# Gathering finished pairs of expert rows during the last MoE blocks of a hybrid decoder layer

## The chip, the core and the metric

The kernel runs on one core of one Trainium2 chip. The metric is the device time of one execution in microseconds (us), given as the median of several runs. Five engines work side by side: TensorE (PE in the rows, PEld its weight loads), VectorE (DVE), ScalarE (ACT), GpSimd (POOL) and SyncE (SP, which here only issues transfers). The transfers themselves are carried by 16 DMA engines. A transfer issued by SP goes through one queue, an indexed one (indirect) issued by POOL through another.

## What is computed

The reference is one decoder layer over 1024 prompt tokens and 64 sample tokens (1088 rows of 1024 floats). The part that matters here is the end of it, a mixture of 32 experts in which each token goes to the best two experts of its best group:

```
g_idx = top_k(softmax(xt @ rg_w + rg_b), 1)                     # one of 4 groups
v2, e_idx = top_k(le_sel, 2)                                    # two of its 8 experts
w2 = softmax(v2) * p_top
hg, hu = xt @ w_gate[e], xt @ w_up[e]                           # 1024 -> 128
out = sum over the two experts of (silu(hg) * hu * gate) @ w_down[e]
x = x + out
y = x * rsqrt(mean(x * x) + 1e-6) * g_final
```

## The kernel before

All rows are in 9 tiles: tiles 0 to 7 hold 128 prompt tokens each, tile 8 (`LAST`) the 64 sample tokens. The first two thirds of the time go to projections and mixers: 16 column pieces of `w_in` are loaded by SP into two `raw` buffers, each when the piece two before it has been split (`load_piece`), and TensorE reads the split pieces from a ring of four. Then each tile is projected back and routed. VectorE writes, for every expert, the list of its tokens.

The experts run in `NB` = 29 blocks. Blocks 0 to 7 are experts 0 to 7. The other 24 experts are put in an order by their size (`pos`, a position 0 to 23 for each): ten small ones run in pairs, two to a block, then the large ones, then the rest, one to a block. `place(r)` says which expert position block `r` does. For each block, POOL gathers the tokens' rows from `scratch_h` into `xg`, TensorE multiplies them, ScalarE and VectorE each copy half of the result into `outb`, and POOL scatters `outb` to the DRAM tensor `scratch_out` (`scatter`, L1217). That tensor has 2 x 1088 rows of 4 KB, the two rows of a token next to each other, so a token's pair is 8 KB in one piece. A block with up to 128 rows is scattered in one of four sizes, chosen on POOL by branches (`by_size`). SP loads the weights of an expert (3 x 512 KB) into one of eight slots as soon as the slot's last user is done. VectorE does small pieces of bookkeeping between the blocks (`between`, keyed by the block's number).

After block 28 comes code for experts with more rows than fit, which runs zero times on these inputs: a loop of three rounds on TensorE, ScalarE, VectorE and SP (`Fori`), and on POOL `over_from(0)`, one branch around 19 nested levels of code. When both scatter semaphores are full, POOL does a `memset` whose end is `moe_done` (L1270). That releases SP, which loads the pair rows of all nine tiles, whole, in the order `FINAL` = 8, 0, 1, 2, 3, 4, 7, 5, 6 (L652, 0.5 MB for tile 8, 1 MB for each other one).

A tile's end is the same whoever does it: its own rows plus each of its two expert rows times a gate, then a norm. For tiles 8, 1, 3, 7 VectorE adds (`add_experts`, L1961, two instructions). For tiles 0, 2, 4, 5, 6 TensorE adds (`PE_TILES`: first the own rows by the identity, `own_rows`, L2479, then eight matmuls with diagonal gate matrices `dg`, L2496); the own rows of tile 6 come between tiles 4 and 5, as they need the banks of tile 0. ScalarE squares and takes the root in the order of `FINAL` (L669 or L1096, then L1081), VectorE scales (`final_norm`, L1969 and L1974), and SP stores the tile. VectorE's order is written out by hand: add 8, norm 8, add 1, norm 0, 1, 2, add 3, add 7, norm 3, 4, 7, 5, 6.

Of the kernel before, what the change touches and what calls it, by code (L numbers as in the profile page):

```python
# [27 lines left out]
P = 128  # L28
# [30 lines left out]
DVE_TILES = [8, 1, 3, 7]  # L59
NPAR = 31 + 3 + 4  # L60
# [103 lines left out]
def build_layer(nc, a):  # L164
    with ExitStack() as ctx:
# [128 lines left out]
        order = at("order", [P, 8, REST], o_state + 2304)  # L294
        eid = at("eid", [1, REST], o_state + 3072, I32)
# [26 lines left out]
        eidx = sb("eidx", [P, 2, 2])  # L322
# [41 lines left out]
            "eid_ready", "perm_ready", "ones_ready", "place_ready", "table_added", "cols_ready", "idx_ready", "ov_ready", "xg_zero", "three_gathers",  # L364
# [139 lines left out]
        def _(sp):  # L504
# [58 lines left out]
            for g in range(4):  # L563
                q = g % 2 * 64
                sp.dma_start(pw[q:q + 64, g // 2, q:q + 64], a["pool_w"][0, g])\
                    .then_inc(s["pw_in"], 16)
            for p in range(2, NPIECE):
                load_piece(p)
                if p == 5:

                    sp.wait_ge(s["wsT_masked"], 1)
                    for b in range(SB):
                        sp.dma_start(wsb[b * ST:(b + 1) * ST, :, b * ST:(b + 1) * ST],
                                     wsT[0:ST, :, 0:ST]).then_inc(s["wsb_in"], 16)
                if p == 4:

                    sp.wait_ge(s["h_ready"], TILES)
                    sp.dma_start(gain[:], a["g_ffn"].to_broadcast([P, D]))\
                        .then_inc(s["gain_ffn_in"], 16)
                    sp.dma_start(lng[:], a["ln_d_g"].to_broadcast([P, W])).then_inc(s["ln_d_in"], 16)  # L580
                    sp.dma_start(lnb[:], a["ln_d_b"].to_broadcast([P, W])).then_inc(s["ln_d_in"], 16)
# [10 lines left out]
            def expert_block(i, j, e, first=False):  # L592

                if not first:

                    sp.wait_ge(s["d_done"], i * LAP + max(done_in(NE + j - LAP), NB + j - LAP) + 1)
                load_expert(i, j, e, first)
# [507 lines left out]
        def _(pool):  # L1105
# [106 lines left out]
            def scatter(b, index):  # L1212
# [8 lines left out]
                if is_pair(b):  # L1221
# [12 lines left out]
            pool.wait_ge(s["xg_zero"], XG)  # L1234
            for k in range(2):
                pool.wait_ge(h2_stored[k], 16 * ((TILES + 1 - k) // 2))
            pool.wait_ge(s["idx_ready"], 1)
            def gather_over(o):

                with pool.If(total > o):  # L1240
# [5 lines left out]
                    gather(NB + o, gcol[:, o:o + 1], scol[:, o:o + 1], NB + o - 3)  # L1246

            for b in range(-XG, NB + 1):
# [14 lines left out]
                if b >= 1:  # L1263
                    scatter(b - 1, columns(b - 1)[1])

# [20 lines left out]
            over_from(0)  # L1286


        @block.vector
        def _(dve):  # L1290
# [314 lines left out]
            def route(i):  # L1605
# [25 lines left out]
                do(v.tensor_copy(eidx[q, z, :], j8[q, 0:2]))  # L1631

            def places(i):
# [17 lines left out]
                do(stt(col[q, :], eidx[q, z, :], float(CAPB), rhi[q, :], ALU.mult, ALU.add))  # L1651
# [57 lines left out]
            do(v.memset(flat[:], 0.0))  # L1709
            for i in range(LAST):  # L1710
# [154 lines left out]
            def overflow_counts():  # L1865

                do(ts(ovi[:], carry[0:1, :], float(P - 1), None, ALU.add))
# [5 lines left out]
                do(ts(few[0:1, :], pos[0:1, :], LIGHT - 0.5, None, ALU.is_le))  # L1873
                do(stt(again[:, FIX:NE], rest[0:1, :], 64.0, few[0:1, :], ALU.is_gt, ALU.mult))
                do(ts(few[0:1, :], pos[0:1, :], LIGHT + LARGE - 0.5, -1.0, ALU.is_ge, ALU.add))
                do(stt(run[0:1, :], rest[0:1, :], P + 64.5, few[0:1, :], ALU.is_le, ALU.mult))
                do(stt(few[0:1, :], pos[0:1, :], LIGHT - 0.5, run[0:1, :], ALU.is_ge, ALU.mult))
                do(stt(n_e[:, FIX:NE], few[0:1, :], 1.0, n_e[:, FIX:NE], ALU.add, ALU.mult))
                do(tt(n_e, n_e, again[:, 0:NE], ALU.add))
                do(v.tensor_tensor_scan(incl, ones[0:1, 0:NE], n_e, 0.0, ALU.mult, ALU.add))  # L1880
# [3 lines left out]
            def overflow_sums():  # L1884

                do(tt(otmp[:], incl.unsqueeze(1).broadcast_to(grid), iob[:].unsqueeze(2).broadcast_to(grid),
# [3 lines left out]
            def overflow_lists():  # L1890

                do(tt(otmp[:], otmp[:], ovm[:].unsqueeze(1).broadcast_to(grid), ALU.mult))
# [8 lines left out]
            def overflow_blocks():  # L1901
# [4 lines left out]
                do(v.tensor_copy(ovt[:, 2 * OVER:2 * OVER + 1], incl[:, NE - 1:NE]), s["ov_ready"])  # L1906

            between = {1: expert_order, 2: light_columns, 3: extra_columns, 4: other_columns,
# [47 lines left out]
            def add_experts(i):  # L1956

                n = rows(i)
                dve.wait_ge(pair_in[i], 16)
# [32 lines left out]
        def _(pe):  # L1992
# [494 lines left out]
            for t, i in enumerate(PE_TILES):  # L2487
# [3 lines left out]
                pe.wait_ge(pair_in[i], 16)  # L2491
# [38 lines left out]
```

## Time and profile before

| | |
|---|---|
| median of 3 runs | 609.39 us (609.37 to 610.42) |
| the profiled execution's own time | 608.55 us |
| its span, first to last instruction | 606.5 us |
| TensorE busy | 571.4 us, 94% of the span |
| VectorE busy | 439.9 us, 73% |
| POOL busy | 88.5 us, 15% |
| moved by DMA | 111.27 MB, mean 183 GB/s |

Busy time is an average over stages. In the stage of the experts TensorE is busy nearly all the time; in the last 40 us no engine is, and what counts there is which transfer or result comes last. The span ends with the last store. The execution's own time is 2.05 us more than its span; the median of the runs is 0.84 us above the profiled execution.

### The profile page before, as it was taken

The numbers are of one execution on the slowest core, as the hardware profiler recorded it, in microseconds if no ns is written. First come the engines' busy times: TensorE is split into PE (matmuls) and PEld (weight loads), VectorE is DVE, ScalarE is ACT, GpSimd is POOL, SyncE is SP. The second block draws the span as 40 slices with busy tenths as digits, with TensorE's granted clock in tenths as the row PEclk, the third lists the DMA queues.
The fourth block names the chain that finished last, engine by engine and source line by source line (L and its number), as shares of the span: only waits on it lengthen the run. The fifth ranks groups of instructions, "written<-read, shape, count | busy, mean of one in ns | idle before, by whom it ended". The sixth has DMA issues, their size and how long they took to land.

```text
span 606.5 us, 9765 instructions
## 1 busy us (share of the span) xinstructions
PE 571.4 (94%) x3401; PEld 473.4 (78%) x3401; DVE 439.9 (73%) x749; ACT 242.2 (40%) x389; POOL 88.5 (15%) x136
## 2 busy tenths in 40 slices
PE   8899999999999999899999995899997999999775
PEld 6799999997899889688888874777654768887222
DVE  4937997999999696746666658899731667786285
ACT  6642112222212427322222116576322567775443
POOL 4300000200000000100000000433331334431000
PEclk9999999999999999999999997899998999999889
DMA  8761210131112202455422107699989999962697
GB/s 317 150 123 38 69 36 1 36 93 35 36 36 79 105 36 69 114 203 198 157 80 93 54 36 247 215 332 404 392 329 412 407 352 395 394 241 97 209 421 299
DMA packets 52598, 111.27 MB, mean 183 GB/s; under 512 B 10867, under 2 KB 29176, under 8 KB 51449
## 3 DMA queue, kind: packets, MB, share of 16 engines
q1 hardware_dynamic: 44773, 92.18, 43.2%
q0 software_dynamic: 7168, 17.84, 8.2%
q8 instruction: 30, 0.49, 0.3%
q10 hardware_dynamic: 596, 0.50, 0.3%
q14 instruction: 31, 0.25, 0.1%
HBM read 96.36 MB, written 21.86 MB: 195 GB/s over the span
## 4 chain that ended last, share of the span: by engine, by line
PE 51%; DVE 17%; DMA 7%; issue 3%; ACT 2%; SPq 1%; POOL 0%; POOLq 0%; DVEq 0%; ACTq 0%
PE ps L2259 14%; PE ps L2081 9%; PE ps L2425 6%; PE ps L2364 3%; PE ps L2386 3%; PE ps L2400 3%; PE ps L2401 3%; PE ps L2402 3%; DMA at_opair_p<-scratch_out 3%; DMA at_wlater<-in_expert_w_down 3%; DVE at_mixP L1360 3%; PE ps L2496 2%; PE ps L2323 2%; DVE at_hT L1319 1%; DVE at_lnsq L1546 1%
## 5 line engine op out<-in xcount | busy, mean ns | idle before, releaser
L2081 PE MATMUL ps<-at_hT,at_ring 128*128 128x384 f32 x936 | 165.5, 333 | 0.0
L2081 PEld LDWEIGHTS ps<-at_hT,at_ring 128*128 128x128 f32 x936 | 155.9, 188 | 5.1 <-issue 5.0
L2259 PE MATMUL ps<-at_hT,at_mring 128*128 128x512 f32 (+1 forms) x432 | 102.7, 393 | 2.0 <-DVE at_mring L1514 1.3
L2259 PEld LDWEIGHTS ps<-at_hT,at_mring 128*128 128x128 f32 (+1 forms) x432 | 77.3, 182 | 21.3 <-DVE at_mring L1514 1.7
L1360 DVE SCALAR_TENSOR_TENSOR at_mixP<-at_uc,at_par,at_mixP 128x1024 f32<-128x1024 f32 x60 | 77.1, 1285 | 2.1
L2400 PE MATMUL ps<-at_whi,at_hTm 128*128 128x256 f32 x176 | 51.0, 290 | 0.0
L2402 PE MATMUL ps<-at_whi,at_hTm_lo 128*128 128x256 f32 x176 | 49.1, 279 | 0.0
L2364 PEld LDWEIGHTS ps<-sb_ident,at_xg 128*128 128x128 f32 x232 | 29.3, 192 | 18.2 <-issue 15.2
L1795 DVE TENSOR_TENSOR at_wlater_lo<-at_wlater,at_whi 128x1024 fp32r<-128x1024 f32 x30 | 36.7, 1225 | 6.0 <-ACT at_whi L988 5.1
L2425 PE MATMUL ps<-at_wlater,at_actT 128*128 128x512 f32 (+1 forms) x92 | 38.0, 597 | 0.7 <-ACT at_actT L1003 0.7
L988 ACT ACTIVATE at_whi<-at_wlater 128x1024 fp32r<-128x1024 f32 x30 | 31.6, 1055 | 7.3 <-PE ps L2402 6.5
L669 ACT ACTIVATE at_wk<-at_x 128x1024 f32<-128x1024 f32 (+1 forms) x13 | 13.8, 1059 | 51.4 <-DVE at_x L1586 44.8
L2364 PE MATMUL ps<-sb_ident,at_xg 128*128 128x128 f32 x232 | 31.6, 279 | 2.5 <-DMA at_xg<-scratch_h,at_gidxs 2.3
L1777 DVE TENSOR_TENSOR at_hTm_lo<-ps,at_hTm 128x1024 fp32r<-128x1024 f32 x21 | 25.7, 1223 | 11.2 <-ACT at_hTm L969 11.1
L2401 PE MATMUL ps<-at_wlater_lo,at_hTm 128*128 128x256 f32 x120 | 33.6, 280 | 0.0
L2400 PEld LDWEIGHTS ps<-at_whi,at_hTm 128*128 128x128 f32 x176 | 33.1, 188 | 0.2
L2402 PEld LDWEIGHTS ps<-at_whi,at_hTm_lo 128*128 128x128 f32 x176 | 33.0, 188 | 0.0
L1217 POOL DMA_INDIRECT scratch_out<-at_outb,at_sperm x21 | 20.8, 989 | 69.2 <-DVE at_outb L1765 69.2
L1202 POOL DMA_INDIRECT at_xg<-scratch_h,at_gperm x21 | 26.2, 1246 | 20.5 <-issue 14.4
L1765 DVE COPY at_outb<-ps 128x512 f32<-128x512 f32 x29 | 19.9, 686 | 10.6 <-PE ps L2425 10.5
L1012 ACT ACTIVATE at_outb<-ps 128x512 f32<-128x512 f32 x29 | 17.3, 597 | 25.5 <-PE ps L2425 23.2
L2127 PE MATMUL ps<-at_ring,at_hT 128*128 128x256 f32 (+1 forms) x216 | 25.9, 282 | 0.0
(324 smaller groups left out, 919.2 us busy)
## 6 DMA issues: line engine op xcount, KB each, us to landing
at_wlater<-in_expert_w_gate SPq DMA_DIRECT2D x20, 512.0 KB, 11.1
at_wlater<-in_expert_w_up SPq DMA_DIRECT2D x20, 512.0 KB, 12.8
at_wlater<-in_expert_w_down SPq DMA_DIRECT2D x20, 512.0 KB, 15.4
at_raw<-in_w_in SPq DMA_DIRECT2D x16, 512.0 KB, 4.0
at_opair_p<-scratch_out SPq DMA_DIRECT2D x8, 1024.0 KB, 14.7
at_wfirst<-in_expert_w_gate SPq DMA_DIRECT2D x12, 512.0 KB, 9.0
at_wfirst<-in_expert_w_up SPq DMA_DIRECT2D x12, 512.0 KB, 10.0
at_wfirst<-in_expert_w_down SPq DMA_DIRECT2D x12, 512.0 KB, 12.5
```

The lines of the kernel that those rows point to most:

```text
L988: nc.scalar.activation(whi[h][:], half(wexp(w), h), ACT.Copy).then_inc(s[f"w_hi{h}"], 1)
L1202: g.indirect_dma_start(xg[0:n, b % XG, :], None, hs, bass.IndirectOffsetOnAxis(ap=index[0:n, :], axis=0), bounds_check=last_token, oob_is_ ...
L1360: do(stt(y, x, par[:, c, k:k + 1], y, ALU.mult, ALU.add))
L1795: v.tensor_tensor(half(wexp_lo(w), h), half(wexp(w), h), whi[h][:].bitcast(F32), ALU.subtract).then_inc(s[f"w_lo{h}"], 1)
L2081: mm = pe.matmul(ps[:, bank + r, 0:t1 - t0], w[:, wpart, k * P:(k + 1) * P], hT[:, hpart, k, t0:t1], start=(m, wpart, hpart) == (0, 0, 0), ...
L2127: mm = pe.matmul(b[0:n, 0:W].rearrange("p (s c) -> p s c", s=2), hT[:, hpart, k, i * P:i * P + n], vw[:, :, wpart, k * P:(k + 1) * P], sta ...
L2259: mm = pe.matmul(ps[0:n, b + r, :], mring[:, 1 - i % 2, mpart, k * P:k * P + n], wo[:, wpart, k, r * 512:(r + 1) * 512], start=(c, mpart, ...
L2364: mm = pe.transpose(rows_psum(b)[:, k // 4, k % 4 * P:(k % 4 + 1) * P], xg[:, j % XG, :].rearrange("p (q k) -> p k q", k=KC)[:, k, :], ide ...
L2400: pe.matmul(out, x, high, start=k == 0, stop=False)
L2401: pe.matmul(out, x, low, start=False, stop=False)
L2402: mm = pe.matmul(out, x_low, high, start=False, stop=k == KC - 1)
L2425: mm = pe.matmul(ps[n, bank + r, :], actT[:, j % 2, n], wexp(place(j, t or 0))[:, q:q + 512], start=True, stop=True)
```

## The change

The pair rows of six tiles (8, 0, 1, 2, 3, 7) now come through POOL's queue, each in two indexed gathers: an early one for the tokens whose two experts are both done, and a late one for the others. Three waves of two tiles are issued after the scatters of blocks 24, 25 and 26, and wait for the scatters up to block 23, 24 and 25. A list holds for each token its number, or a number beyond the bound, for which nothing is moved: `soon` for the early gathers, `later` for the late ones. The other three tiles (4, 5, 6, `WHOLE`) are loaded whole by SP, once the late gather of tile 1 has landed.

For this, the chosen experts of all tiles are kept (`eidx`), VectorE works out the lists in three new pieces after blocks 11, 12 and 13, the counts of rows over the limit are worked out on all partitions and not on one, SP copies the inputs over `scratch_out` once during the pieces (`fill_out`, ten copies DRAM to DRAM, 8.5 MB), and blocks 25 to 28 are scattered with 128 rows without the branches. The buffers of the pairs and of `dg` move to slots that are free by then.

```
+EARLY = [[8, 0], [1, 2], [3, 7]]
+WAVES = len(EARLY)
+WHOLE = [4, 5, 6]
+def wave_after(n):
+    return NB - 3 - WAVES + n
...
             for p in range(2, NPIECE):
                 load_piece(p)
+                if 5 <= p < 14:
+                    fill_out(p - 5)
...
-            sp.wait_ge(s["moe_done"], 1)
-            for i in FINAL:
-                n = rows(i)
-                src = orow[2 * i * P:2 * (i * P + n), :].rearrange("(t k) d -> t (k d)", k=2)
-                sp.dma_start(opair(i)[0:n, :], src).then_inc(pair_in[i], 16)
+            sp.wait_ge(pair_in[FINAL[2]], 32)
+            for i in WHOLE:
+                src = orow[2 * i * P:2 * (i + 1) * P, :].rearrange("(t k) d -> t (k d)", k=2)
+                sp.dma_start(opair(i), src).then_inc(pair_in[i], 16)
...
-                if is_pair(b):
+                if is_pair(b) or NB - 4 <= b < NB:
                     move(P)
...
+            def pair_rows(i, index):
+                g.indirect_dma_start(opair(i), None, pairs,
+                                     bass.IndirectOffsetOnAxis(ap=index[:, i:i + 1], axis=0),
+                                     bounds_check=last_token, oob_is_err=False).then_inc(pair_in[i], 16)
+            def early_pairs(n):
+                pool.wait_ge(s["turns_ready"], 1)
+                for k in range(2):
+                    pool.wait_ge(scat[k], 16 * ((wave_after(n) + 2 - k) // 2))
+                for i in EARLY[n]:
+                    pair_rows(i, soon)
...
                     scatter(b - 1, columns(b - 1)[1])
+                if 0 <= b - 2 - wave_after(0) < WAVES:
+                    early_pairs(b - 2 - wave_after(0))
...
             over_from(0)
+            pool.wait_ge(s["moe_done"], 1)
+            for i in FINAL:
+                if i not in WHOLE:
+                    pair_rows(i, later)
...
+            def pair_turns():
+                do(v.memset(turn[:, 0:FIX], 0.0))
+                do(v.tensor_copy(turn[:, FIX:NE], pos))
+                shape = [P, TILES * 2, NE]
+                do(tt(w, io32[:].unsqueeze(1).broadcast_to(shape), chosen, ALU.is_equal))
+                do(tt(w, w, turn[:].unsqueeze(1).broadcast_to(shape), ALU.mult))
+            def pair_latest():
+                do(v.tensor_reduce(latest[:], both[:], AX_X, ALU.add))
+                do(tt(done_by[:], latest[:, :, 0], latest[:, :, 1], ALU.max))
+                do(ts(no_over[:], incl[:, NE - 1:NE], 0.5, None, ALU.is_le))
+                do(ts(token[:], pid[:, :, 0], 0.5, -0.5, ALU.mult, ALU.add))
+            def pair_lists():
+                for n in range(WAVES):
+                    last_turn = place(wave_after(n)) - FIX + 0.5
+                    for i in EARLY[n]:
+                        do(ts(done_by[:, i:i + 1], done_by[:, i:i + 1], last_turn, no_over[:], ALU.is_le,
+                              ALU.mult))
+                do(stt(later[:], done_by[:], float(NONE), token[:], ALU.mult, ALU.add))
+                do(ts(done_by[:], done_by[:], -float(NONE), float(NONE), ALU.mult, ALU.add))
+                do(tt(soon[:], done_by[:], token[:], ALU.add), s["turns_ready"])
...
-                pe.wait_ge(pair_in[i], 16)
+                pe.wait_ge(pair_in[i], 16 if i in WHOLE else 32)
```

On POOL, the program's end reads as follows before the change; the first row stands in the last scatter's choice of a size, and the last rows are the end of `over_from`.

```order
L1217 DMA scratch_out<-at_outb,at_sperm 2176x1024
L1194 UNCONDITIONAL_BRANCH
...
L1192 COMPARE_AND_BRANCH
L1217 DMA scratch_out<-at_outb,at_scol 2176x1024
L1192 UNCONDITIONAL_BRANCH
L1217 DMA scratch_out<-at_outb,at_scol 2176x1024
L1194 UNCONDITIONAL_BRANCH
L1270 MEMSET at_gcol 128x1
L1280 UNCONDITIONAL_BRANCH
```

The same place after the change begins with the last scatter (now without branches) and `all_scattered`. The branch L1322 is row 854 of POOL's program and leads around `over_from` to row 1588, the first late gather.

```order
L1244 DMA scratch_out<-at_outb,at_sperm 2176x1024
L1330 COMPARE_AND_BRANCH
L1316 MEMSET at_gcol 128x1
L1330 UNCONDITIONAL_BRANCH
L1322 COMPARE_AND_BRANCH
...
L1316 MEMSET at_gcol 128x1
L1326 UNCONDITIONAL_BRANCH
L1280 DMA at_opair_a<-scratch_out,at_later 128x2048 x4
L1280 DMA at_opair_b<-scratch_out,at_later 128x2048 x2
L173 UNCONDITIONAL_BRANCH
```

Nothing stood behind `over_from` before; six gathers stand there now.

On SP, the last transfers before the change are nine loads and nine stores.

```order
L640 REGISTER_ALU
L640 COMPARE_AND_BRANCH
L652 DMA at_opair_s<-scratch_out 64x2048
L652 DMA at_opair_p<-scratch_out 128x2048 x8
L498 DMA out_y_sample<-at_x_86 64x1024
L498 DMA out_y_prompt<-at_x_86 128x1024 x8
```

After it, three loads are left (L679), and they wait for tile 1's late gather and no longer for `moe_done`.

```order
L668 REGISTER_ALU
L668 COMPARE_AND_BRANCH
L679 DMA at_opair_b<-scratch_out 128x2048 x3
L515 DMA out_y_sample<-at_x_86 64x1024
L515 DMA out_y_prompt<-at_x_86 128x1024 x8
```

Six of nine loads have left SP's queue for POOL's. Earlier on SP, among the pieces, the copies (L589) stand behind the piece loads (L541):

```order
L541 DMA at_raw<-in_w_in 128x8x128
L589 DMA scratch_out<-in_x_prompt 16x16384
L599 DMA at_wsb<-at_wsT 8x4x8 x8
L541 DMA at_raw<-in_w_in 128x8x128
L589 DMA scratch_out<-in_x_prompt 16x16384
L541 DMA at_raw<-in_w_in 128x8x128
L589 DMA scratch_out<-in_x_prompt 16x16384
```

So a piece's load now follows the copy that was issued with the piece before it.

## Rows read from the trace of the kernel before

**Rows 1.** Chain that ended last, in order of time, last 45 us: start, us, what
```profile
567.31 0.09 POOL at_gcol L1270
...
570.11 16.12 DMA at_opair_p<-scratch_out
...
591.68 1.72 PE ps L2479 x4
593.39 6.88 PE ps L2496 x16
```

**Rows 2.** Timeline of VectorE at the end: start, us, what, [idle before <-releaser]
```profile
567.00 0.19 DVE L1947 TENSOR_REDUCE sb_stage<-sb_stage 128x9 f32<-128x36 f32 x1 [4.45 <-issue]
...
572.59 2.59 DVE L1961 SCALAR_TENSOR_TENSOR at_x<-at_opair_s,sb_gates,at_x 64x1024 f32<-64x1024 f32 x2 [4.51 <-DMA at_opair_s<-scratch_out]
576.86 0.15 DVE L1969 RECIPROCAL sb_rs<-sb_rs 64x1 f32<-64x1 f32 x1 [1.68 <-ACT sb_rs L1081]
...
585.60 0.16 DVE L1969 RECIPROCAL sb_rs<-sb_rs 128x1 f32<-128x1 f32 x1 [1.48 <-ACT sb_rs L1081]
...
598.47 0.16 DVE L1969 RECIPROCAL sb_rs<-sb_rs 128x1 f32<-128x1 f32 x1 [1.54 <-ACT sb_rs L1081]
...
601.90 0.16 DVE L1969 RECIPROCAL sb_rs<-sb_rs 128x1 f32<-128x1 f32 x1 [1.95 <-ACT sb_rs L1081]
602.10 1.28 DVE L1974 SCALAR_TENSOR_TENSOR at_x<-ps,sb_rs,sb_gain 128x1024 f32<-128x1024 f32 x1
```

**Rows 3.** Timeline of TensorE at the end
```profile
565.64 8.99 PE L2479 MATMUL ps<-at_x,sb_ident 128*128 128x512 f32 x16 [3.82 <-issue]
574.92 3.70 PE L2496 MATMUL ps<-at_opair_p,at_dg 128*128 128x512 f32 x8 [0.29 <-DMA at_opair_p<-scratch_out]
580.26 3.70 PE L2496 MATMUL ps<-at_opair_p,at_dg 128*128 128x512 f32 x8 [1.64 <-DMA at_opair_p<-scratch_out]
586.28 5.40 PE L2496 MATMUL ps<-at_opair_p,at_dg 128*128 128x512 f32 x8 [2.32 <-DMA at_opair_p<-scratch_out]
```

**Rows 4.** Stretches: start:end, length, busy us of PE, PEld, DVE, ACT, POOL, clock, DMA, GB/s
```profile
551.00:563.30 12.30, 10.08 (x52) 6.48 (x50) 5.89 (x8) 4.69 (x9) 2.81 (x3) 1.00 0.27 97
...
580.30:586.30 6.00, 3.68 (x9) 1.42 (x9) 4.22 (x7) 2.85 (x6) 0.00 (x0) 1.00 1.03 425
586.30:594.00 7.70, 7.70 (x14) 3.32 (x15) 7.45 (x8) 3.61 (x7) 0.00 (x0) 0.78 1.00 412
```

**Rows 5.** Timeline of POOL: the first gathers of the experts' stage, and the last scatters
```profile
380.12 1.31 POOL L1202 DMA_INDIRECT at_xg<-scratch_h,at_gidxs  x1 [10.35 <-DVE at_gidxs L1746]
381.74 1.31 POOL L1202 DMA_INDIRECT at_xg<-scratch_h,at_gidxs  x1 [0.30 <-issue]
...
560.50 0.92 POOL L1217 DMA_INDIRECT scratch_out<-at_outb,at_sperm  x1 [3.04 <-DVE at_outb L1765]
563.34 0.92 POOL L1217 DMA_INDIRECT scratch_out<-at_outb,at_sperm  x1 [1.92 <-DVE at_outb L1765]
```

**Rows 6.** Issue to landing: first the two gathers of [rows 5], then L652's nine loads
```profile
DMA to landing us min/median/max: 4.4/4.5/4.7
...
DMA to landing us min/median/max: 5.0/13.2/22.0
```

**Rows 7.** Timeline of VectorE in blocks 7 to 14
```profile
432.68 0.77 DVE L1888 TENSOR_REDUCE at_ovb<-at_otmp 1x19 f32<-1x608 f32 x1
...
466.36 0.29 DVE L1757 TENSOR_TENSOR at_actv<-at_sg,ps 128x128 f32<-128x128 f32 x1 [7.45 <-ACT at_sg L995]
...
469.92 1.23 DVE L1777 TENSOR_TENSOR at_hTm_lo<-ps,at_hTm 128x1024 fp32r<-128x1024 f32 x1 [1.46 <-ACT at_hTm L969]
...
477.10 1.22 DVE L1777 TENSOR_TENSOR at_hTm_lo<-ps,at_hTm 128x1024 fp32r<-128x1024 f32 x1 [0.79 <-ACT at_hTm L969]
```

**Rows 8.** The pieces: two loads of L524 (60 to 71 us), and ScalarE's waits for them
```profile
L524 SPq DMA_DIRECT2D at_raw<-in_w_in x2: 590/600/611, 62.4 to 69.0; - x2
...
ACT at_ring L694 <- DMA at_raw<-in_w_in: 8.5, 2, 5.3
```

More of the change, by code:

```diff
@@ L294, in build_layer @@
         order = at("order", [P, 8, REST], o_state + 2304)
+        both = at("both", [P, TILES, 2, NE], o_state)
+        turn = at("turn", [P, NE], o_state + 2304)
+        latest = at("latest", [P, TILES, 2], o_state + 2304 + 192)
+        done_by = at("done_by", [P, TILES], o_state + 2304 + 288)
+        token = at("token", [P, TILES], o_state + 2304 + 384)
+        soon = at("soon", [P, TILES], o_state + 2304 + 480, I32)
+        later = at("later", [P, TILES], o_state + 2304 + 672, I32)
+        no_over = at("no_over", [P, 1], o_state + 2304 + 736)
         eid = at("eid", [1, REST], o_state + 3072, I32)
@@ L566, in _, with fill_out @@
                     .then_inc(s["pw_in"], 16)
+            def fill_out(n):
+                r = n * 256 % NP
+                for src, at_, count in ((a["x_prompt"][0, r:r + 256, :], n * 256, 256),) if n < 8 else tuple(
+                        (a["x_sample"].rearrange("b t d -> (b t) d"), 2 * NP + h * NS, NS) for h in range(2)):
+                    sp.dma_start(orow[at_:at_ + count, :], src).then_inc(s["out_filled"], 16)
             for p in range(2, NPIECE):
                 load_piece(p)
+                if 5 <= p < 14:
+                    fill_out(p - 5)
                 if p == 5:
@@ L1709, in _ @@
             do(v.memset(flat[:], 0.0))
+            do(v.memset(eidx[:], 0.0))
             for i in range(LAST):
@@ L1865, in overflow_counts @@
             def overflow_counts():
-                do(ts(ovi[:], carry[0:1, :], float(P - 1), None, ALU.add))
+                do(ts(ovi[:], carry[:], float(P - 1), None, ALU.add))
                 do(ts(ovi[:], ovi[:], 7, None, ALU.logical_shift_right))
@@ L1872, in overflow_counts @@
                 do(v.memset(again[:], 0.0))
[L1873 to L1878, printed above, removed]
+                do(ts(few, pos, LIGHT - 0.5, None, ALU.is_le))
+                do(stt(again[:, FIX:NE], rest, 64.0, few, ALU.is_gt, ALU.mult))
+                do(ts(few, pos, LIGHT + LARGE - 0.5, -1.0, ALU.is_ge, ALU.add))
+                do(stt(run, rest, P + 64.5, few, ALU.is_le, ALU.mult))
+                do(stt(few, pos, LIGHT - 0.5, run, ALU.is_ge, ALU.mult))
+                do(stt(n_e[:, FIX:NE], few, 1.0, n_e[:, FIX:NE], ALU.add, ALU.mult))
                 do(tt(n_e, n_e, again[:, 0:NE], ALU.add))
-                do(v.tensor_tensor_scan(incl, ones[0:1, 0:NE], n_e, 0.0, ALU.mult, ALU.add))
+                do(v.tensor_tensor_scan(incl, ones[:, 0:NE], n_e, 0.0, ALU.mult, ALU.add))
                 do(tt(ovm[:], n_e, again[:, 1:NE + 1], ALU.add))
```

41 lines of the change are left out of this document (24 added, 17 removed).

## The prediction

> **What bounds the kernel now.** I read the chain of waits first, from its end backwards. The span of 606.5 us ends with the store of tile 6, 3.1 us behind VectorE's last scaling (602.10 + 1.28 = 603.38) [rows 2]. Ahead of that stand TensorE's sums of tiles 5 and 6 and the own rows of tile 6, and ahead of tile 4's sum 16.12 us of the pair loads [rows 1]. The reader is to see that nothing but these loads stands between `moe_done` (the memset, 567.31) and TensorE's start on tile 4. TensorE's timeline says the same: idle for 0.29, 1.64 and 2.32 us before tiles 0, 2 and 4, each time for a pair load [rows 3]. From 580.3 to 586.3 the DMA engines are busy for all of their time at 425 GB/s [rows 4]: the end is bound by 8.5 MB through the DMA engines. Ahead of it, from 551 to 563.3, they are busy 0.27 of the time [rows 4]. So the change takes bytes from a full stretch to a nearly empty one. VectorE comes next: from its first add at 572.59 to 603.38 it has 30.8 us, of which 1.68, 1.48, 1.54 and 1.95 us stand before roots [rows 2]. That leaves about 24.0 us of work.
>
> **How much moves.** I ran the reference's routing on its inputs and the kernel's ordering of experts over it. Of the 704 tokens in the six tiles, 481 have both experts done when their wave is sent (35, 75, 91, 83, 91, 106 in the order 8, 0, 1, 2, 3, 7) and 223 are late (29, 53, 37, 45, 37, 22). At 8 KB a pair the late gathers carry 1.8 MB; with 3 MB for the whole tiles the end moves 4.8 MB in place of 8.5.
>
> **The end, step by step.** `moe_done` stays at 567.4, the end of the memset [rows 1]. Behind it POOL must branch around `over_from`, some 730 rows of its program, before it can issue a gather. The trace has no such branch on POOL. Bounds: nothing, and the 4.45 us that VectorE spent from its last copy to its next instruction, over its empty loop of three rounds [rows 2]; TensorE spent 3.82 us on its own [rows 3]. POOL has one branch where they have three rounds, so I take the middle, 2.2. The Trainium skill ("Runtime: NRT & Kernel Launch", Instruction fetch mechanics) says that a taken branch out of the two pages held must first fetch the page it leads to; by it alone the price can't be nothing, and the trace agrees in that two engines idle there.
>
> The first late gather (tile 8) is issued at 567.4 + 2.2 = 569.6. Two gathers in a row start 1.62 us apart (380.12, 381.74) [rows 5], so tile 0 follows at 571.2 and tile 1 at 572.8. Landing took 4.4 to 4.7 us from the issue for 128 rows of 4 KB [rows 6], and at the last scatter, issued at 563.34 and waited for by the memset, 3.9 [rows 1, 5]. For 29 to 53 rows of 8 KB (0.24 to 0.43 MB) I take 4.0 to 4.2, with 3.5 and 5.5 as bounds. Tile 8 lands at 573.6, against 572.59 before: a late gather saves nothing for the first tile. Tile 1 lands at 577.0.
>
> Then SP issues the three whole loads. Alone, the 0.5 MB of tile 8 landed in 5.0 us [rows 6]; another 0.5 MB at 425 GB/s adds 1.3, and the late gathers of tiles 2, 3 and 7 (0.85 MB, 2 us of DMA time) go on beside it, for which I add half, 1.0. Tile 4 lands at 577.1 + 7.3 = 584.4, against 586.2 before: 1.8 us earlier. The Trainium skill ("DMA: Bandwidth & Descriptors", Anatomy of one DMA) gives 2.0 us plus bytes at 436 GB/s for one DMA. An estimate by that page: a late gather lands in 2.7 us and 1 MB in 4.4, and tile 4 would be some 3.4 us earlier still; the rows are longer for both.
>
> Two chains lead on from there. **TensorE's:** before, from the start of tile 4 to the end of the span it took 606.5 - 586.28 = 20.2 us. In it are 5.40 us for tile 4's eight matmuls where tiles 0 and 2 took 3.70 [rows 3], in a stretch with a granted clock of 0.78 of full [rows 4], a mean of the levels 2.4 and 1.2 GHz. If the clock falls again, the span ends at 584.4 + 20.2 = 604.6; if it doesn't, 1.7 us earlier. TensorE idled 2.3 us before tile 4 then and would again (tile 2's pairs land at 578.5, its sum ends at 582.2), but it was less busy before that; I take the middle, 603.7. **VectorE's:** 573.6 + 24.0 + 1.7 for the root of tile 8 + 0.1 = 599.4, plus 3.1 for the store = 602.5. With the pairs on hand its other three stalls are gone. The later chain counts: 603.7, 2.8 us less than 606.5. TensorE's first own rows end at 574.63 whatever comes (565.64 + 8.99) [rows 3]. Five sums of 3.5, the own rows of tile 6 with 1.7 [rows 1], a root with 1.6, a norm with 1.5 and the store come behind: even instant pairs don't end below some 600.
>
> **What is hidden.** VectorE's lists. A reduce of 608 elements took 0.77 us [rows 7], so the piece after block 11 costs about 2 us (two operations on 576 elements), the next 1.4, the last some 1.9 (nine small ones). The first falls ahead of the 7.45 us in which VectorE idles until 466.36, the second into the 1.46 us ahead of 469.92; the third has only 0.79 us ahead of 477.10 and moves that instruction by about 1.1 [rows 7]. That one makes the left-over half of a block's rows, which TensorE reads a block later, so I count nothing; if the cover is gone it costs 1.1. The wider counts have the same elements per partition, so no more time.
>
> The early gathers are issued behind scatters that stand over 5 us apart. Only the last wave touches something: its two issues, from 557.5 on, end at about 560.7, and the scatter of block 27 was at 560.50 [rows 5]. Its 1.6 MB are 3.8 us of DMA time in the same queue as the last two scatters. I count 0.2, within 0 and 1.5. Taking the branches away saves nothing, as POOL waited 1.92 us for VectorE at the last scatter [rows 5].
>
> The copies. 1 MB at 425 GB/s takes 2.5 us, or 5 if it counts twice, read and written. The shortest gap that I found between a load with a copy behind it and the next load is 62.4 to 69.0, 6.6 us [rows 8]. Cost nothing, while a copy stays under that.
>
> **Sum.** 606.5 - 2.8 + 0.2 = a span of 603.9, and 605.9 with the 2.05 us around it, 2.6 below the profiled 608.55. The median of the runs is 0.84 above that execution, so 609.39 - 2.6 = 606.8. A measurement of this kernel tells 0.2% from no change, 1.2 us.
>
> **Rivals.**
> A, the forecast: TensorE's chain through the whole loads ends last, 1.2 to 4.2 us gained, median 605.2 to 608.2. Chance 0.55.
> B: the branch costs 0 to 1, or the transfers land up to 3 us sooner. Tile 4 is in by 582, and VectorE's chain or TensorE's floor ends last, at 600.9 to 602.2: 4.3 to 5.6 gained, median 603.8 to 605.1. For it: one branch, and DMA engines with little else to do. Against: two engines idle about 4 us at that place. 0.22. The skill's fit of a DMA, above, leads here.
> C: the branch costs as much as VectorE's 4.45. Tile 4 lands at 586.7 and the end is at 606.9, less up to 1.7 by the clock. Within 0.2%: no change, 608.2 to 610.6. 0.14.
> D, slower: the copies hold the pieces. ScalarE waits twice for a load already, 8.5 us in all [rows 8]; there each us beyond 6.6 a copy is passed on. At 10 us a copy that is 2 x 3.4 = 6.8 lost, less the gain of 2.6: median about 613.6. It decides from 8.5 us a copy on. Against: the copies' bytes are few for 6.6 us. 0.07.
> The last 0.02: the lists come out empty, so that nothing is early, and 8.5 MB go at the end again, six tiles by POOL and with the branch ahead: about 2 us slower.
>
> **How the numbers follow.** Faster by over 0.2%: A and B, 0.77. Same: C and a little of D, 0.15. Slower: 0.08. The range takes in A and most of B and C: 604.0 to 609.0.
>
> **What would show it.** On the span after: tile 8's first add near 573.6 and tile 4's sum near 584.4 for the two landings; between POOL's memset and its first late gather, the price of the branch (2.2). DMA well over 0.27 busy from 551 to 563. No idle on TensorE during the pieces and none new in blocks 12 to 15. The prediction is wrong if the first late gather comes before 568.5 or after 571.5, if the first whole load takes under 5 or over 9 us, or if `moe_done` is displaced by more than 1 us.

## The result, and the profile after

| | before | after |
|---|---|---|
| median of 20 runs each | 609.38 us (607.73 to 611.85) | 612.56 us (610.71 to 614.88) |
| ratio | | 1.0055, 95% interval 1.0042 to 1.0068 |
| profiled execution | 608.55 us, span 606.5 us | 613.24 us, span 611.3 us |

The change made the kernel 3.2 us slower, where 2.6 us of gain were forecast; 612.56 lies outside the range of 604.0 to 609.0. The profiled pair differs by 4.7 us, 1.5 more than the medians.

The page of after, its queues (packets, megabytes, share of the 16 DMA engines):

```profile
q1 hardware_dynamic: 44293, 95.33, 43.9%
q0 software_dynamic: 8960, 23.61, 11.1%
```

So the early gathers and the copies' bytes are there. Between 200 and 345 us the two agree (TensorE busy for 143.0 and 143.4 us, DMA share 0.33 in both), and between 30 and 200 us only the copies' bytes show: TensorE was busy for 168.68 us of those 170 before and is for 168.69 now, while the DMA engines' share rose from 0.20 to 0.31. Columns as in [rows 4]:

```profile
30.00:200.00 170.00, 168.69 (x1104) 162.45 (x1104) 148.23 (x177) 44.07 (x88) 4.58 (x4) 1.00 0.31 106
...
550.00:555.00 5.00, 5.00 (x35) 4.04 (x34) 4.32 (x5) 3.66 (x6) 2.83 (x3) 1.00 0.78 265
555.00:560.00 5.00, 5.00 (x34) 3.99 (x34) 3.30 (x5) 2.41 (x5) 2.46 (x4) 1.00 0.85 276
560.00:565.00 5.00, 4.15 (x12) 1.56 (x11) 0.98 (x2) 1.04 (x3) 3.64 (x4) 1.00 0.91 297
565.00:570.00 5.00, 0.00 (x0) 0.00 (x0) 1.62 (x6) 0.60 (x1) 0.99 (x1) 1.00 0.87 313
```

The stretch ahead of `moe_done`, 0.27 busy before [rows 4], is 0.78 to 0.91 busy now, and at 265 to 313 GB/s, not 425. POOL's timeline there, against [rows 5]: L1244 is a scatter, L1280 a gather of pairs, `soon` the early and `later` the late ones.

```profile
559.59 1.02 POOL L1244 DMA_INDIRECT scratch_out<-at_outb,at_sperm  x1 [1.93 <-DVE at_outb L1816]
560.91 1.02 POOL L1280 DMA_INDIRECT at_opair_b<-scratch_out,at_soon  x1 [0.30 <-issue]
562.24 1.00 POOL L1280 DMA_INDIRECT at_opair_b<-scratch_out,at_soon  x1 [0.30 <-issue]
563.58 1.01 POOL L1244 DMA_INDIRECT scratch_out<-at_outb,at_sperm  x1 [0.34 <-issue]
566.90 0.99 POOL L1244 DMA_INDIRECT scratch_out<-at_outb,at_sperm  x1 [2.31 <-DVE at_outb L1816]
573.76 0.10 POOL L1316 MEMSET at_gcol<- 128x1 int32 x1 [5.87 <-DMA scratch_out<-at_outb,at_sperm]
577.13 1.03 POOL L1280 DMA_INDIRECT at_opair_a<-scratch_out,at_later  x1 [3.27 <-issue]
578.47 1.01 POOL L1280 DMA_INDIRECT at_opair_a<-scratch_out,at_later  x1 [0.31 <-issue]
```

Two things are to be seen. The last scatter (566.90) is waited for until 573.76, 6.9 us, where it was 4.0 from issue to memset before [rows 1, 5]. And 3.27 us of "issue", a wait for nothing that the profile shows, stand between the memset and the first late gather: the way around `over_from`.

VectorE and TensorE of after, against [rows 2, 3]:

```profile
565.42 0.69 DVE L1816 COPY at_outb<-ps 128x512 f32<-128x512 f32 x1 [2.63 <-DMA scratch_out<-at_outb,at_sperm]
...
581.87 2.59 DVE L2040 SCALAR_TENSOR_TENSOR at_x<-at_opair_a,sb_gates,at_x 64x1024 f32<-64x1024 f32 x2 [13.05 <-DMA at_opair_a<-scratch_out,at_later]
586.13 0.15 DVE L2048 RECIPROCAL sb_rs<-sb_rs 64x1 f32<-64x1 f32 x1 [1.68 <-ACT sb_rs L1108]
...
593.82 0.16 DVE L2048 RECIPROCAL sb_rs<-sb_rs 128x1 f32<-128x1 f32 x1 [0.42 <-ACT sb_rs L1108]
...
606.89 1.28 DVE L2053 SCALAR_TENSOR_TENSOR at_x<-ps,sb_rs,sb_gain 128x1024 f32<-128x1024 f32 x1
```

```profile
571.27 10.02 PE L2558 MATMUL ps<-at_x,sb_ident 128*128 128x512 f32 x16 [6.38 <-issue]
583.35 8.83 PE L2575 MATMUL ps<-at_opair_a,at_dg 128*128 128x512 f32 x16 [2.06 <-DMA at_opair_a<-scratch_out,at_later]
592.02 3.60 PE L2575 MATMUL ps<-at_opair_b,at_dg 128*128 128x512 f32 x8
```

The first add comes at 581.87, not 572.59. From there all goes as hoped: of VectorE's stalls ahead of roots only tile 8's 1.68 us and 0.42 us of tile 2's are left, and TensorE doesn't wait for tile 4. From the first add to the end of the span it is 29.4 us, against 33.9. So 4.5 us are won behind the first add and 5.7 lost between the last scatter and it (15.0 us against 9.25). The other 3.6 us of the pair's 4.8 came before the last scatter's issue (566.90 against 563.34), 3.1 of them already before the scatter of block 24 (548.49 against 545.41).

### The profile page after: what moved, and what is told of

Its sections match the earlier page's. It is cut to its first block, busy times and chain, and to the rows that moved or that the text cites. A ratio compares the mean times of both kernels' runs of the same rounds, so it can differ in the third digit from the quotient of the medians.

```text
span 611.3 us, 9766 instructions
## 1 busy us (share of the span) xinstructions
PE 574.2 (94%) x3401; PEld 476.9 (78%) x3401; DVE 444.4 (73%) x767; ACT 242.3 (40%) x389; POOL 101.8 (17%) x148
## 4 chain that ended last, share of the span: by engine, by line
PE 48%; DVE 21%; DMA 6%; issue 4%; ACT 2%; POOL 1%; SPq 0%; POOLq 0%; DVEq 0%; ACTq 0%
PE ps L2338 14%; PE ps L2160 8%; PE ps L2504 5%; PE ps L2465 3%; PE ps L2443 3%; DVE at_mixP L1410 3%; DMA at_wlater<-in_expert_w_down 2%; PE ps L2480 2%; PE ps L2479 2%; PE ps L2481 2%; PE ps L2402 2%; PE ps L2575 1%; DMA scratch_out<-at_outb,at_sperm 1%; DVE at_hT L1369 1%; DVE at_wlater_lo L1846 1%
## 5 line engine op out<-in xcount | busy, mean ns | idle before, releaser
L1015 ACT ACTIVATE at_whi<-at_wlater 128x1024 fp32r<-128x1024 f32 x30 | 31.6, 1055 | 7.4 <-PE ps L2481 5.7
L1244 POOL DMA_INDIRECT scratch_out<-at_outb,at_sperm x21 | 21.1, 1004 | 63.6 <-DVE at_outb L1816 63.3
```

Of the source, the lines that this page charges most:

```text
L1015: nc.scalar.activation(whi[h][:], half(wexp(w), h), ACT.Copy).then_inc(s[f"w_hi{h}"], 1)
```

## Experiments

All changed kernels keep the copies, the lists and the 128-row scatters unless said otherwise. The table has the medians of 12 runs each (20 of after, 6 of t4) and the ratios (each against runs of before on its own chip), and from each profiled execution the length of three pieces: last scatter's issue to the first add on tile 8; first add to the end of the span; and both with the four scatters ahead, from the scatter of block 24. The last leaves out what happened earlier. The three pieces come from one profiled execution each.

| kernel | median | ratio [95%] | scatter 28 to add | add to end | scatter 24 to end |
|---|---|---|---|---|---|
| before | 609.38 | | 9.3 | 33.9 | 61.1 |
| t7 before, fixed scatters | 609.70 | 1.0005 [0.9987, 1.0023] | 8.6 | 34.0 | 60.6 |
| t1 old end | 609.07 | 0.9976 [0.9956, 0.9995] | 9.5 | 31.6 | 58.9 |
| **after** | 612.56 | 1.0055 [1.0042, 1.0068] | 15.0 | 29.4 | 62.8 |
| t2 late gathers ahead of the branch | 609.47 | 0.9993 [0.9972, 1.0015] | 12.4 | 29.1 | 59.8 |
| t3 no third wave, 3 and 7 late by POOL | 613.37 | 1.0053 [1.0025, 1.0081] | 11.6 | 34.4 | 65.0 |
| t4 whole loads at once | 616.32 | 1.0101 [1.0072, 1.0130] | 18.0 | 30.9 | 67.5 |
| t5 third wave behind scatter 28, no branch | 608.32 | 0.9982 [0.9961, 1.0003] | 12.2 | 29.2 | 59.7 |
| t6 the same with the branch | 611.83 | 1.0030 [1.0012, 1.0049] | 16.3 | 29.3 | 63.4 |
| t8 two waves, five whole, no branch | 609.31 | 0.9993 [0.9973, 1.0013] | 8.8 | 31.9 | 58.9 |
| t9 the same, SP sooner | 610.83 | 1.0016 [0.9996, 1.0036] | 8.6 | 33.2 | 59.9 |
| t10 as t8 with the branch | 612.57 | 1.0037 [1.0016, 1.0058] | 11.5 | 32.6 | 62.5 |
| t11 third wave of tile 3 alone, no branch | 606.95 | 0.9956 [0.9933, 0.9979] | 9.0 | 29.6 | 56.6 |
| t12 the same behind scatter 28 | 606.07 | 0.9937 [0.9912, 0.9961] | 8.8 | 29.2 | 56.4 |

### Front or end: t1 and t7

t1 gives the changed kernel its old end back: no early or late gathers, nine loads by SP. It keeps the new places of the pair buffers.

```diff
-                if 0 <= b - 2 - wave_after(0) < WAVES:
-                    early_pairs(b - 2 - wave_after(0))
...
-            for i in FINAL:
-                if i not in WHOLE:
-                    pair_rows(i, later)
...
-            sp.wait_ge(pair_in[FINAL[2]], 32)
-            for i in WHOLE:
+            sp.wait_ge(s["moe_done"], 1)
+            for i in FINAL:
```

> The changed kernel with the end of before: no early or late gathers, SP loads all nine tiles whole at moe_done; the copies over scratch_out, the lists and the 128-row scatters stay. Theory Q (the loss of 3.2 us is made at the end: the last scatters land late behind the early gathers, then POOL's branch, then the late gathers): only 0 to 1.5 us over before, 609.4 to 610.9. Rival U (the loss is made upstream by copies and lists): 612 to 613, like the changed kernel.

609.07 us, ratio 0.9976: not slower than before. So copies, lists and wider scatters don't make the loss; it is made at the end. t7 is the kernel before with the last four scatters fixed at 128 rows:

```diff
-                if is_pair(b):
+                if is_pair(b) or NB - 4 <= b < NB:
                     move(P)
```

> The kernel before with one part of the change alone: the scatters of the last four blocks always carry 128 rows, so that the branches by size in front of them are gone. If the 0.24 per cent that the old end with the new upstream won came from these branches, this kernel is 1 to 1.5 us faster than before (ratio 0.9975); if it is chance or comes from elsewhere, within 0.1 per cent of before. If the larger transfers cost something, slower by up to 1 us.

No difference, so the branches by size are worth nothing here, and t1's small gain isn't theirs. t7's profile shows something else: its scatter of block 24 is at 548.15, 2.7 us later than before's, with before's own front. So most of the 3.1 us by which the profiled after was late there is what two executions of one front can differ by. The granted clock differed as well: from 380 to 400 us TensorE was granted 0.95 of full in the profiled before, 0.82 in t7 and 0.85 in after. Over all twelve kernels with the new front, the difference of medians less the difference of the last column (before and t7 averaged, 60.8) lies between about -1 and +2.3 with a mean of 0.7, and is 1.1 for t7. The front's cost can't be told from nothing.

t1's end is 2.3 us shorter than before's behind the first add. Before and t7 both have 5.40 us for tile 4's sum at a lowered clock [rows 3, 4]; t1 has 3.70 three times. It differs in its buffers' places and in where ScalarE's `dg` lies; which of these does it was not looked into.

### The branch: t2

The late gathers are issued inside the block that gives `moe_done`, ahead of the branch around `over_from`:

```diff
             with pool.If(total < 1):
                 all_scattered(NB)
+                late_pairs()
             over_from(0)
-            pool.wait_ge(s["moe_done"], 1)
-            for i in FINAL:
-                if i not in WHOLE:
-                    pair_rows(i, later)
```

> The changed kernel with the six late gathers issued inside the block of moe_done, ahead of the branch around over_from. Theory Q: the 3.27 us between memset and first late gather shrink to some 0.4, VectorE's chain starts 2.9 us sooner, 609.6 to 610.3. Rival U: the branch is covered by the late start of TensorE's own rows, no gain, 612 to 613.

```profile
565.54 1.00 POOL L1244 DMA_INDIRECT scratch_out<-at_outb,at_sperm  x1 [2.25 <-DVE at_outb L1821]
572.93 0.10 POOL L1316 MEMSET at_gcol<- 128x1 int32 x1 [6.38 <-DMA scratch_out<-at_outb,at_sperm]
573.30 1.03 POOL L1280 DMA_INDIRECT at_opair_a<-scratch_out,at_later  x1 [0.27 <-POOL at_gcol L1316]
```

The 3.27 us of "issue" are 0.27, and the ratio goes from 1.0055 to 0.9993, 3.8 us. The last scatter is still waited for 7.4 us, so this part of the loss stands by itself. Two more pairs on one chip each price the branch: t6 less t5 is 3.5 us, t10 less t8 3.3.

### The whole loads: t4

SP waits for `moe_done` instead of for tile 1's rows.

```diff
-            sp.wait_ge(pair_in[FINAL[2]], 32)
+            sp.wait_ge(s["moe_done"], 1)
```

> The changed kernel with SP's three whole loads issued at moe_done and not behind tile 1's late gather. Theory Q: VectorE's chain from tile 8's late gather ends last, so earlier whole loads bring nothing, and tile 8 may land up to 2 us later beside them: 612.5 to 614.5. My prediction's chain (TensorE waits for tile 4) would give 2 to 4 us less, 608.5 to 610.5.

616.32 us. The late gather of tile 8 (issued at 575.91) lands 8.3 us behind its issue, not 4.7. The 3 MB ahead of it are in another queue, and still it has to wait: from 573 to 580 us the profile has no packet of POOL's queue at all, while SP's queue moves 401 to 459 GB/s from 575 on. Holding SP back is worth it: 2.8 us by the ratios, 4.7 by the last column.

### The third wave: t3, t5, t6

t3 sends no third wave; the late gathers fetch all rows of tiles 3 and 7.

```diff
-EARLY = [[8, 0], [1, 2], [3, 7]]
+EARLY = [[8, 0], [1, 2]]
...
+                for i in (3, 7):
+                    do(ts(done_by[:, i:i + 1], done_by[:, i:i + 1], 0.0, None, ALU.mult))
```

> The changed kernel without its third wave: tiles 3 and 7 come whole by the late gathers, tiles 8, 0, 1, 2 as in the changed kernel. Theory Q: the last scatter lands 3.9 us from its issue and not 6.9, and the half us that the scatter of block 28 waited goes too: 3.0 to 3.5 us less, 609.0 to 609.6, unless the 1.5 MB more at the end take it back. Rival U: no difference, 612 to 613.

The last scatter lands in 3.5 us, 3.4 sooner, and the first add follows 11.6 us behind it, not 15.0. But the time is no better. TensorE of t3:

```profile
580.00 7.13 PE L2577 MATMUL ps<-at_opair_a,at_dg 128*128 128x512 f32 x16 [1.46 <-DMA at_opair_a<-scratch_out,at_later]
592.18 5.65 PE L2577 MATMUL ps<-at_opair_b,at_dg 128*128 128x512 f32 x8 [5.04 <-DMA at_opair_b<-scratch_out]
```

The rows of 3 and 7 are now moved beside the whole tile 4, which TensorE needs first, and it waits for 5.04 us. What the wave cost in front, its absence cost behind. t5 therefore keeps the rows early but sends them behind the last scatter, with the branch gone by the edit of t2; t6 does so with the branch. In both, the late gathers of tiles 3 and 7 wait for their early ones.

```diff
-                if 0 <= b - 2 - wave_after(0) < WAVES:
+                if 0 <= b - 2 - wave_after(0) < WAVES - 1:
                     early_pairs(b - 2 - wave_after(0))
+            early_pairs(WAVES - 1)
             def all_scattered(n):
```

> The version with the late gathers ahead of the branch, and besides the third early wave (tiles 3 and 7) issued behind the last block's scatter instead of behind scatter 26; the late gathers of 3 and 7 wait for their early ones. Theory of the queue (the two last scatters were late because they stood in POOL's queue behind 1 MB of early gathers): the last scatter lands in 3.5 to 4.0 us as with the old end, not in 7.4, the memset comes at about 569.3, the first late gather at 569.6, tile 8's first add at about 574.4 (577.95 with the waves ahead), and the time is about 606.0 us, range 605 to 607.5, ratio 0.993. Rival, contention (the early rows compete with the scatter for the same DMA engines wherever they stand in the queue): the scatter still takes 6 us or more, and the time stays near 609. Rival, TensorE's chain through the whole tile takes over: the first add is sooner, but the whole tile 4 lands late and the time falls by less than 2 us.

> The changed kernel with the third early wave issued behind the last block's scatter, the branch still ahead of the late gathers. Theory of the queue: 3.4 us less than the changed kernel's 612.6, so about 609.2 (608.3 to 610.5), the same as before; the memset at about 569.5 and the first late gather some 3.3 us behind it. If the two prices (queue and branch) add, this kernel minus the one with both removed is 3.1 to 3.5 us. Rival, contention: no gain against the changed kernel, 612 or more.

(The megabyte in these texts is too little: the wave's 197 rows of 8 KB are 1.6 MB, as the prediction had it.) POOL of t5, and VectorE's first add:

```profile
565.56 0.97 POOL L1244 DMA_INDIRECT scratch_out<-at_outb,at_sperm  x1 [2.13 <-DMA scratch_out<-at_outb,at_sperm]
566.84 1.04 POOL L1280 DMA_INDIRECT at_opair_b<-scratch_out,at_soon  x1 [0.30 <-issue]
568.18 1.01 POOL L1280 DMA_INDIRECT at_opair_b<-scratch_out,at_soon  x1 [0.30 <-issue]
569.19 0.12 POOL L1318 MEMSET at_gcol<- 128x1 int32 x1
569.58 0.99 POOL L1280 DMA_INDIRECT at_opair_a<-scratch_out,at_later  x1 [0.27 <-POOL at_gcol L1318]
```

```profile
577.76 2.59 DVE L2049 SCALAR_TENSOR_TENSOR at_x<-at_opair_a,sb_gates,at_x 64x1024 f32<-64x1024 f32 x2 [10.25 <-DMA at_opair_a<-scratch_out,at_later]
```

My theory that the scatter's place in the queue was what cost fell by half. The scatter is in on time (by 569.19, 3.6 us), but now tile 8's late gather takes 8.2 us, not 4.7, and scatter to add is 12.2 us against 12.4. Whatever comes right behind the wave pays some 3.5 us; moving the wave merely changes who does. The gain of 3 us that I expected of t5 didn't come: against t2 it is 0.7, inside the intervals.

t6 came at 611.83, not 609.2, for the same reason. It also shows this:

```profile
569.02 0.12 POOL L1318 MEMSET at_gcol<- 128x1 int32 x1
576.85 0.99 POOL L1280 DMA_INDIRECT at_opair_a<-scratch_out,at_later  x1 [7.70 <-issue]
```

With the wave's rows in flight the branch takes 7.70 us; without them it took 3.27, 3.36, 3.10 and 3.12 (after, t3, t4, t10).

### Fewer bytes ahead, an order by need: t8, t9, t10

Two waves, and tiles 3, 4, 7, 5, 6 whole by SP in the order in which the end needs them. t8 and t9 have the edit of t2, so no branch stands ahead; t10 has the branch.

```diff
-EARLY = [[8, 0], [1, 2], [3, 7]]
+EARLY = [[8, 0], [1, 2]]
...
-WHOLE = [4, 5, 6]
+WHOLE = [3, 4, 7, 5, 6]
```

> Late gathers ahead of the branch, two early waves only (tiles 8, 0, 1, 2, behind scatters 24 and 25), and the other five tiles (3, 4, 7, 5, 6) loaded whole by SP in the order in which they are needed, once tile 1 has landed. Theory (what costs at the end is every byte that POOL's queue carries ahead of tile 8's late rows; with the third wave gone nothing stands there, and the five whole loads, ordered by need, land in time): last scatter 3.5 us, memset about 569.3, first add at about 574.4, VectorE's chain 24.5 to 26 us behind it, last norm at about 599.5, time 605.5 us, range 604 to 607, ratio 0.992 to 0.994. Rival, bandwidth (the run with tiles 3 and 7 gathered late had its whole tile 4 at 592): tile 4 lands after 588, TensorE's chain ends last, and the time is 608 to 611. Rival, nothing: the order of the whole loads doesn't keep them in order on the 16 engines and tile 3 is late for VectorE, time 607 to 609.

> The same, but SP starts the five whole loads as soon as tile 8 has landed, some 1.5 to 3 us sooner. If the loads' landing bounds anything, this is 0.5 to 2 us faster than the version that waits for tile 1. If the late rows of tiles 0, 1 and 2 are slowed by 1 MB loads beside them, as tile 8's were when the whole loads went at once (8.3 us against 4.7), VectorE stalls before tile 1 and the time is 1 to 3 us longer. If VectorE's chain bounds and has slack at tile 1, no difference (within 0.5 us).

> The changed kernel with two early waves and the five whole loads in the order of need, the branch still ahead of the late gathers. Theory that the two prices are separate: 3.1 to 3.5 us slower than the same without the branch, so about 608.9, a little faster than before. With nothing in the DMA queues while the branch is taken, POOL stands 3.1 to 3.5 us behind the memset (7.7 with the wave in flight). Rival: the branch's price disappears in slack, and the two are equal.

The first half of t8 is as expected, 8.8 us from scatter to add. The second is not: 31.9 us, where versions with a third wave have some 29.2. Its stretches from 580 to 590, and TensorE at tile 4:

```profile
580.00:585.00 5.00, 5.00 (x12) 1.90 (x10) 4.71 (x6) 2.85 (x6) 0.00 (x0) 1.00 1.01 421
585.00:590.00 5.00, 3.46 (x9) 1.63 (x9) 4.61 (x6) 1.41 (x3) 0.00 (x0) 1.00 1.01 426
```

```profile
586.58 3.70 PE L2580 MATMUL ps<-at_opair_b,at_dg 128*128 128x512 f32 x8 [1.54 <-DMA at_opair_b<-scratch_out]
```

The DMA engines are busy all the time, and TensorE waits 1.54 us for a whole load. Of the rival "bandwidth" the time came, and TensorE's chain does end last (VectorE waits 1.50 us before its last norm), though tile 4 was in at 586.6 and not after 588. The sum, 609.31, is that of t2 by another route. t9 starts the five loads as soon as tile 8 is in: late rows of tile 2 then land late (TensorE waits 2.12 us for them, VectorE 4.17 for the root behind), and it is 1.5 us slower. The expectation had put the stall before tile 1. t10 shows the branch's 3.3 us once more, and that it is not slack.

### One tile fewer in the third wave: t11, t12

The two routes bound each other: 1.6 MB ahead of tile 8's rows cost 3.5 us, five whole tiles behind cost 2.7. In between lies a third wave with tile 3 alone (91 rows, 0.75 MB) and tile 7 whole, again with the edit of t2.

```diff
-EARLY = [[8, 0], [1, 2], [3, 7]]
+EARLY = [[8, 0], [1, 2], [3]]
...
-WHOLE = [4, 5, 6]
+WHOLE = [4, 7, 5, 6]
```

> Late gathers ahead of the branch; the third early wave holds tile 3 alone (up to 1 MB) at its place behind scatter 26, and tile 7 is loaded whole by SP with 4, 5 and 6 in the order of need. Theory of the queue, now as a line through two points (no third wave: last scatter 3.5 us; both tiles: 7.4): with half the rows the last scatter takes 5.0 to 5.8 us, tile 8's first add comes at 575.5 to 576.5 with scatter 28 at about 566, VectorE's chain 25 us behind it, time 607.5 to 608.5, ratio about 0.998. Rival, a fixed cost (a transfer waits once for a queue that is not empty, however much is in it): the scatter takes 7 us or more and the time stays at 609.4. Rival, the whole loads bound (4 MB behind tile 1): TensorE stalls and the time is 609.

> The same with tile 3's early rows behind the last scatter. Theory (the bytes cost the same wherever they stand ahead of tile 8's late rows): the scatter takes 3.5 us and tile 8's late gather lands after 5.9 to 6.7 us, between 4.7 with nothing ahead and 8.2 with both tiles ahead; first add at 575.5 to 576.5, time equal to the version with the rows ahead of the scatter within 1 us, 607 to 608.5. If it is faster by more than 1 us, the lateness of the scatter itself is what costs.

Both are faster than before, t11 by 0.44% and t12 by 0.63%, and with that than after, which is 0.55% slower than before (they were not run beside after itself). They do better than their forecasts of 607.5 to 608.5 and 607 to 608.5, which came from a line through two points. POOL of t11:

```profile
564.55 1.00 POOL L1244 DMA_INDIRECT scratch_out<-at_outb,at_sperm  x1 [1.83 <-DVE at_outb L1821]
568.60 0.10 POOL L1316 MEMSET at_gcol<- 128x1 int32 x1 [3.05 <-DMA scratch_out<-at_outb,at_sperm]
568.97 1.04 POOL L1280 DMA_INDIRECT at_opair_a<-scratch_out,at_later  x1 [0.27 <-POOL at_gcol L1316]
```

4.05 us for the last scatter, not 5.0 to 5.8: half the wave costs little, 0.5 us over t3. In t12, too, tile 8's late gather lands in 4.7 us behind the half wave, not in 5.9 to 6.7. The stretches of 2 us around the scatter say why. First t2 (scatter 28 at 565.54), then t11 (at 564.55):

```profile
561.00:563.00 2.00, 1.37 (x3) 0.68 (x4) 0.50 (x1) 0.57 (x2) 1.65 (x2) 1.00 0.88 287
563.00:565.00 2.00, 0.61 (x2) 0.00 (x0) 0.69 (x1) 0.60 (x1) 0.29 (x1) 1.00 1.02 301
565.00:567.00 2.00, 0.00 (x0) 0.00 (x0) 0.52 (x3) 0.00 (x0) 1.00 (x1) 0.79 0.91 311
567.00:569.00 2.00, 0.00 (x0) 0.00 (x0) 0.41 (x3) 0.00 (x0) 0.00 (x0) 0.50 0.78 307
```

```profile
561.00:563.00 2.00, 1.95 (x4) 0.68 (x4) 0.00 (x0) 0.00 (x1) 1.01 (x1) 1.00 0.85 272
563.00:565.00 2.00, 0.04 (x1) 0.00 (x0) 0.69 (x1) 0.60 (x1) 0.45 (x1) 1.00 0.68 262
565.00:567.00 2.00, 0.00 (x0) 0.00 (x0) 0.93 (x5) 0.00 (x0) 0.55 (x1) 1.00 0.48 178
567.00:569.00 2.00, 1.06 (x2) 0.56 (x3) 0.00 (x0) 0.15 (x1) 0.13 (x2) 0.73 0.11 43
```

In t2 the DMA engines are still at 300 GB/s on the wave's rows when the scatter comes and for 3 us behind it. In t11 they are emptying. The packets of t2 can be told apart by size, 4 KB for a scatter's row and 8 KB for a pair. The scatter of block 27 was issued at 562.29, but from 564 to 567 us only 2 of the 111 packets of 4 KB and more are rows of a scatter; from 567 to 569 it is 92 of 120. So the rows of the last two scatters moved when the wave's had gone. In t3, without the wave, the rows of block 27's scatter (issued at 562.82) move from 564 on. What costs is the backlog that is left when the urgent transfer is issued, not the bytes that were sent: the three waves are 5.6 us apart, and in after the DMA engines are 0.78 to 0.91 busy from 550 on. Tile 7's 106 rows, 0.87 MB at the 300 GB/s of these rows, are 2.9 us, and between t11 and t2 the scatter's wait differs by 3.3. t12's 0.9 us over t11 is within what their runs scatter by; it was expected within 1 us.

## Why the prediction was wrong, step by step

Right: the lists and copies are hidden and the pieces and blocks unharmed, as far as the runs resolve it (t1; rival D is out); DMA is well over 0.27 busy ahead of `moe_done`; a late gather saves nothing for the first tile; no stall is left on VectorE in front of the whole tiles; the quickest of SP's whole loads landed in 6.3 us, where the forecast had 7.3 for the first. Two of the forecast's own signs of being wrong came up: `moe_done` 6.5 us late, and the first late gather at 577.13.

**The step that failed** is "`moe_done` stays at 567.4", with the 0.2 us counted for the last wave, "within 0 and 1.5". I had the term, 3.8 us of DMA time in the same queue as the last two scatters, and let it vanish into a quiet stretch without adding up what stood in it already. It cost 2.9 us at the memset and 0.5 before, where VectorE's copy into `outb` for block 28 waited 2.63 us for the scatter of block 26, which has the same buffer (in t1 it waited 2.15 us, for TensorE). It was mis-sized in rate, too: I took 425 GB/s, the rate of whole loads [rows 4], for gathered rows that went at 265 to 313.

**The branch**, a term of the sum that was sized too small, took 3.27 us, not 2.2: within the bounds, on the dear side. The Trainium skill ("Runtime: NRT & Kernel Launch", Instruction fetch mechanics) has a taken branch beyond the pages held wait for a fetch; the trace agrees, and t2 removed it.

**The landing** of tile 8's late rows took 4.7 us, not 4.0. The Trainium skill's fit for one DMA ("DMA: Bandwidth & Descriptors", Anatomy of one DMA) gives 2.5 for its 0.24 MB, an estimate by that page; here the measurement decides, with 4.6 to 4.8 us in each of the nine kernels where nothing large stood ahead or beside. The page's fit is for transfers that GpSimd issues; the prediction took it for SP's whole loads as well.

**What was better:** from the first add to the end 29.4 us, where the forecast had 603.9 - 573.6 = 30.3. VectorE's chain ends last, not TensorE's through the whole loads.

The sum, in the profiled span: 3.1 us before the scatter of block 24 (t7 has 2.7 of them with the old front), 0.5 + 2.9 for the wave, 1.1 for the branch, 0.7 for the landing, less 0.9 behind the first add: 7.4, which is 611.3 - 603.9. Against the medians the change's own terms at the end give 4.3 of the 5.8 us by which I missed. The other 1.5 lie ahead of that scatter or between one profiled execution and a median; these runs don't resolve it.

Was the idea wrong? Not as such: its balance was, and its place behind the branch. t12 has the same code with one tile moved to the whole loads, the third wave behind the last scatter and the late gathers ahead of the branch, and it gains 3.9 us where the prediction had 2.6 for the change. Both corrections are in that number. With the branch back, at the 3.3 to 3.8 us that the three pairs price it, some 0.1 to 0.6 us of gain would be left; that is an estimate, and no run has the better balance with the branch.

Not settled: whether the last scatter would have passed the wave from another queue. In t4 a gather waits for the bytes of another queue (8.3 us), so sharing the engines is enough for a delay, but no run has the wave and the scatter in different queues. Early gathers without the copies that fill the rows first were not tried.

## What to carry to other kernels

Moving bytes ahead of a barrier pays only as long as they have drained when the transfer that opens the barrier is issued: sum the backlog wave by wave, at the rate that such gathers have in a trace, and look at what the slack in front of the urgent transfer holds. A step hung behind a program's barrier must also stand in front of every branch over rarely used code. And when two versions that err on opposite sides give the same time, try the one in the middle.

## What the hardware showed that I had not expected

A branch over code costs more when gathered rows are in flight: POOL's took 3.10 to 3.36 us in four kernels and 7.70 in t6, where 1.6 MB had just been issued. The profile has queues of kind instruction, which carried 30 packets each in after, and their packets show where the time goes. In the four kernels the first of them behind the memset ran within 1.4 us (in t4 between 573.6 and 574.0, ahead of nearly all data of SP's loads). In t6 the memset ended at 569.14 and the first ran between 574.4 and 574.8, when the DMA engines had fallen from 0.98 busy (571 to 573) to 0.26 (573 to 575). Those 4 to 5 us more cover the 4.4 that t6's branch took over after's. The profile doesn't name the engine that a packet serves, and no run took this alone.

TensorE agrees. Its "issue" ahead of its own rows, behind its empty loop, is 3.4 to 4.0 us in the ten kernels where the DMA engines had little to do at that time (among them before 3.82, t1 3.82, t3 3.42, t8 3.95), 4.90 in t11, and 5.86, 6.38 and 6.25 in t4, after and t2, where the third wave was in flight. So does ScalarE, ahead of its `dg`: 4.13 in t1 and 3.87 in t12, but 7.35, 7.52 and 8.18 in t4, after and t2. VectorE doesn't: its wait at that place is 1.65 us in t1, after and t2 alike, and 4.45 and 4.58 in before and t7, so it can't be read as a price of the loop alone.

Gathered rows of 8 KB, with scatters between them, kept the DMA engines of after 0.78 to 0.91 busy and moved only 265 to 313 GB/s, where contiguous pairs moved 425 [rows 4]. With almost nothing but gathered rows, from 563 to 565 us in t2, it was 301 GB/s at 1.02.
